# Two fused transformer blocks on one core: a weight split done by the load instead of by VectorE, and another order of work at the start of each feed-forward

## The reference, cut to what matters

```python
def swiglu(x, w_gate, w_up, w_down):
    return (jax.nn.silu(x @ w_gate) * (x @ w_up)) @ w_down

# first mixer: 8 heads, each with 64 columns without and 32 columns with rotation
q = (rms_norm(cq, q_norm_g) @ w_uq).reshape(B, S, MLA_HEADS, MLA_NOPE + MLA_ROPE)

# first block
f1 = swiglu(rms_norm(h, ffn1_pre_g[l]), ffn1_w_gate[l], ffn1_w_up[l], ffn1_w_down[l])
h = h + 0.5 * rms_norm(f1, ffn1_post_g[l])
...
f2 = swiglu(rms_norm(h, ffn2_pre_g[l]), ffn2_w_gate[l], ffn2_w_up[l], ffn2_w_down[l])
h = h + 0.5 * rms_norm(f2, ffn2_post_g[l])
```

## Time and profile before

| what | value |
|---|---|
| median of three runs | 1330.87 us |
| the profiled execution | 1330.87 us, its span 1329.2 us |
| TensorE (PE) busy | 1261.1 us, 95% |
| VectorE (DVE) busy | 789.1 us, 59% |
| ScalarE (ACT) busy | 593.7 us, 45% |
| GpSimd (POOL) busy | 453.0 us, 34% |
| mean granted TensorE clock | 0.970 of full |
| DMA | 206.98 MB, mean 156 GB/s |

### The profile page before, as it was taken

One profiled execution on the slowest core, in us unless ns is written; L12 is line 12 of the kernel. 1 busy time (PEld: TensorE's weight loads), 2 busy tenths in 40 slices (PEclk: granted clock), 3 DMA queues, 4 the chain that ended last, 5 costly groups with the idle time before them and its releaser, 6 DMA issues.

```text
span 1329.2 us, 23438 instructions
## 1 busy us (share of the span) xinstructions
PE 1261.1 (95%) x8728; PEld 1143.4 (86%) x8728; DVE 789.1 (59%) x1135; ACT 593.7 (45%) x976; POOL 453.0 (34%) x252
## 2 busy tenths in 40 slices
PE   6999999898999999999999999988999997999998
PEld 6999999866888999999998888866546797999998
DVE  6677764854974566666352944576324583755555
ACT  5444345525661454444435544343203533655553
POOL 0344334731460533333445642121000374122221
PEclk9999997998999999999969999999999999999999
DMA  8577753423334457777503323222212154455553
GB/s 331 206 267 260 263 197 106 143 95 111 101 107 126 160 182 246 273 280 258 184 17 127 127 94 113 86 89 80 79 63 95 65 176 141 143 180 184 185 178 110
DMA packets 58092, 206.98 MB, mean 156 GB/s; under 512 B 6576, under 2 KB 8240, under 8 KB 57776
## 3 DMA queue, kind: packets, MB, share of 16 engines
q1 hardware_dynamic: 49824, 177.23, 39.5%
q0 software_dynamic: 6912, 25.17, 5.4%
q10 hardware_dynamic: 1296, 3.74, 0.8%
HBM read 205.07 MB, written 1.05 MB: 155 GB/s over the span
## 4 chain that ended last, share of the span: by engine, by line
PE 78%; DVE 10%; DMA 4%; ACT 3%; issue 3%; POOL 1%; SPq 0%; ACTq 0%; DVEq 0%; POOLq 0%
PE psum L589 18%; PE psum L590 17%; PE psum L591 17%; PE psum L560 8%; DMA low<-stream 4%; PE psum L1190 2%; PE psum L915 2%; PE psum L719 2%; PE psum L610 1%; PE psum L1055 1%; ACT parts L1385 1%; POOL own_parts L2684 1%; DVE parts L1979 1%; DVE high L2158 1%; PE psum L1093 1%
## 5 line engine op out<-in xcount | busy, mean ns | idle before, releaser
L589 PE MATMUL psum<-parts 128*128 128x256 f32 x1584 | 452.9, 286 | 23.0 <-DVE parts L1985 11.2
L590 PE MATMUL psum<-parts 128*128 128x256 f32 x1584 | 450.7, 285 | 0.0
L591 PE MATMUL psum<-parts 128*128 128x256 f32 x1584 | 450.5, 284 | 0.0
L589 PEld LDWEIGHTS psum<-parts 128*128 128x128 f32 x1584 | 306.9, 194 | 25.8 <-issue 13.9
L590 PEld LDWEIGHTS psum<-parts 128*128 128x128 f32 x1584 | 306.8, 194 | 0.0
L591 PEld LDWEIGHTS psum<-parts 128*128 128x128 f32 x1584 | 306.6, 194 | 0.0
L1385 ACT ACTIVATE parts<-low 128x1024 fp32r<-128x1024 f32 x198 | 207.7, 1055 | 209.6 <-DMA low<-stream 202.2
L2692 POOL TENSOR_TENSOR parts<-low,parts 128x1024 fp32r<-128x1024 f32 x60 | 158.6, 2644 | 372.3 <-ACT parts L1385 372.3
L2684 POOL TENSOR_TENSOR own_parts<-low,parts 128x1024 fp32r<-128x1024 f32 x76 | 186.4, 2463 | 210.1 <-ACT parts L1457 205.9
L1979 DVE TENSOR_TENSOR parts<-low,parts 128x1024 fp32r<-128x1024 f32 x138 | 175.3, 1276 | 103.7 <-ACT parts L1385 103.4
L560 PE MATMUL psum<-low 128*128 128x256 f32 (+1 forms) x512 | 131.1, 410 | 1.2 <-ACT high L1470 1.2
(11 more groups left out here) (343 smaller groups left out, 1922.9 us busy)
## 6 DMA issues: line engine op xcount, KB each, us to landing
low<-stream SPq DMA_DIRECT2D x334, 512.0 KB, 3.5
high<-conditioning POOLq DMA_DIRECT2D x48, 512.0 KB, 5.8
high<-wuq ACTq DMA_DIRECT2D x1, 1152.0 KB, 11.0
low<-x SPq DMA_DIRECT2D x4, 256.0 KB, 5.6
high<-ctx ACTq DMA_DIRECT2D x1, 1024.0 KB, 6.2
out<-low SPq DMA_DIRECT2D x8, 128.0 KB, 1.8
low<-cst ACTq DMA_DIRECT2D x1, 850.5 KB, 4.7
low<-vec ACTq DMA_DIRECT2D x1, 157.5 KB, 5.9
```

The source lines that it names most:

```text
L589: pe.matmul(out, w_hi[:, cols_], x_hi, start=start, stop=False, **kw)
L590: pe.matmul(out, w_hi[:, cols_], x_lo, start=False, stop=False, **kw)
L591: return pe.matmul(out, w_lo[:, cols_], x_hi, start=False, stop=stop, **kw)
```

## The change

1. `w_nope` and `w_rope` become the two parts of the region of `wuq`, and two loads on ScalarE's queue write them, head by head, straight from memory. A row of `w_nope` is 24 runs of 256 bytes, a row of `w_rope` 24 runs of 128 bytes. VectorE's wait and its two copies go, and so does TensorE's wait for the last counts of `kv_scaled`; TensorE waits for three small loads (48) and not for two (32).
2. The four places of the state-space weights change (`WEIGHT_SUMS`).
3. At the start of each feed-forward, chunk 0: ScalarE's `upper` of tile 6 now stands ahead of `upper_hidden`, and VectorE's `lower` of tile 6 ahead of `lower_hidden`. Chunk 1 had that order already.
4. In feed-forward k = 1, `upper` of tiles 4 and 5 now stand between the root and the table load on ScalarE, and `lower` of tiles 4 and 5 before and after `invert` on VectorE. Before, tile 4 was done amid the first chunk's product, and tile 5 behind it.

```diff
+WEIGHT_SUMS = [ARENA_2["xdt"][0] + 2048, 0, ARENA_2["xdt"][0] + 3072, 0]
+for i in (1, 3):
+    WEIGHT_SUMS[i] = ARENA_2["mk"][0] + (WEIGHT_SUMS[i - 1] + 512 - ARENA_2["mk"][0]) % 1024 + 1024 * (i // 2)
...
-        w_nope = place(ARENA_1["p"][0], 3 * HEADS * NOPE).rearrange("p (k b) -> p k b", k=3)
-        w_rope = place(ARENA_1["va"][0], 3 * HEADS * ROPE_D).rearrange("p (k b) -> p k b", k=3)
+        w_flat, nopes = wuq.rearrange("p a b -> p (a b)"), 3 * HEADS * NOPE
+        w_nope, w_rope = (part.rearrange("p (k b) -> p k b", k=3) for part in (w_flat[:, 0:nopes], w_flat[:, nopes:]))
...
         both_ways = [place(at, 1024).rearrange("p (s t) -> p s t", s=4)
-                     for at in (ARENA_2["xdt"][0] + 2048, ARENA_2["xdt"][0] + 3072,
-                                ARENA_2["mk"][0], ARENA_2["mk"][0] + 1024)]
+                     for at in WEIGHT_SUMS]
...
-            pe.wait_ge(S("small_weights"), 32)
+            pe.wait_ge(S("small_weights"), 48)
...
-            pe.wait_ge(S("kv_scaled"), 4)
...
                     gate(par, par, k > 0, 0)
-                    if par == 0:
-                        upper_hidden(par, FC * k + par)
-                        if k == 1:
-                            upper(1, 5)
                     upper(k, 6 + 3 * par)
-                    if par == 1:
-                        upper_hidden(par, FC * k + par)
+                    upper_hidden(par, FC * k + par)
...
-            act.dma_start(wuq, dram["wuq"]).then_inc(S("small_weights"), 16)
+            w_heads = dram["wuq"].rearrange("p k (h c) -> p (k h) c", h=HEADS)
+            for part, own in ((w_nope, slice(0, NOPE)), (w_rope, slice(NOPE, NOPE + ROPE_D))):
+                act.dma_start(part.rearrange("p k (h c) -> p (k h) c", h=HEADS),
+                              w_heads[:, :, own]).then_inc(S("small_weights"), 16)
...
             take_root("ffn2_pre", D)
+            uppers(1, 4, RING)
             act.preload_act_table(ACT.Silu)
             copy_inverse("ffn2_pre", inv)
-            upper(1, 4)
...
                     product(par, par, 0)
-                    if par == 0:
-                        lower_hidden(par, FC * k + par)
-                        if k == 1:
-                            lower(1, 5)
                     lower(k, 6 + 3 * par)
-                    if par == 1:
-                        lower_hidden(par, FC * k + par)
+                    lower_hidden(par, FC * k + par)
...
-                    if k == 1 and isinstance(f, int) and f == 0:
-                        lower(1, 4)
...
-            dve.wait_ge(S("small_weights"), 32)
-            w_heads = wuq.rearrange("p k (h c) -> p (k h) c", h=HEADS)
-            for part, own in ((w_nope, slice(0, NOPE)), (w_rope, slice(NOPE, NOPE + ROPE_D))):
-                dve.tensor_copy(part.rearrange("p k (h c) -> p (k h) c", h=HEADS), w_heads[:, :, own])\
-                   .then_inc(S("kv_scaled"), 1)
...
             input_sums("ffn2_pre", sq)
+            lower(1, 4)
             invert("ffn2_pre")
+            lower(1, 5)
```

More of the change, by code:

```diff
@@ L200 @@
     ("t0", 512), ("tc", 1024), ("rowm", 512), ("rowl", 256)], END_COMMON)
+WEIGHT_SUMS = [ARENA_2["xdt"][0] + 2048, 0, ARENA_2["xdt"][0] + 3072, 0]
+for i in (1, 3):
+    WEIGHT_SUMS[i] = ARENA_2["mk"][0] + (WEIGHT_SUMS[i - 1] + 512 - ARENA_2["mk"][0]) % 1024 + 1024 * (i // 2)
+assert WEIGHT_SUMS[3] + 1024 <= ARENA_2["mo"][0]
 ATT, _ = regions([("aq", 1024), ("ak", 2048), ("av", 2048), ("after_av", 16), ("mo", 1024), ("ya", 1024)],
@@ L213 @@
 assert END_1 + DC * T <= END_2
-assert 3 * HEADS * NOPE <= 2048 and 3 * HEADS * ROPE_D <= 1024
 HEADS_M = END_2
```

## The result

| | median of the runs | ratio to before, 95% interval |
|---|---|---|
| before, in this comparison | 1332.62 us (1328.63 to 1335.74, 4 runs) | |
| changed | 1346.73 us (1343.40 to 1351.78, 4 runs) | 1.0103 [1.0060, 1.0146] |
| changed, measured again with 9 runs | 1342.48 us, beside 1331.54 for before | 1.0089 [1.0059, 1.0119] |
| forecast | 1335.5 us, range 1329.0 to 1343.0 | 1.0035 |

The change makes the kernel slower by about 1%. The first median lies above the range; that of the 9 runs lies just inside it, at its upper end, and both are two to three times the forecast's +4.6 us away from before. The profiled execution of the changed kernel took 1338.22 us (span 1336.6), less than any of its four timed runs.

The account below looks back on a forecast made before the run. TensorE was taken as the bound, 78% of the chain of work. 1330.87 + 1.8 (loads) + 0 + 2.3 (k = 1) + 0.5 (k = 2) = 1335.5 us, +0.35%, range 1329.0 to 1343.0.

Parts of the forecast that it names:

- The two loads, +1.8 us: Before 36.3 us: new loads delay stream tiles 8 and 9, lengthening TensorE's wait; +1.8 us, bounds -2.2 and +3.4.
- the third rival: ScalarE stands at issuing `w_rope` or `wkr`, ahead of the first feed-forward's root; 6 to 8 us, total 1341; chance 0.12.
- The stream stands still behind the new loads: After 17 us: stream tiles queue behind the new loads' descriptors, SyncE's queue empty for several us, tile 9 late.
- The size of short runs: New loads' 6144 runs at 18 ns each, an estimated 14 for the shorter half; engines held 6.1 us, 3.4 more.
- The rival of dear short runs: Short runs of the new loads cost far more than their bytes, holding engines 11 us; total 1342; chance 0.06.
- The copies, 0: At 270.22 us: VectorE's two copies, 1.42 us, lie wholly in cover of TensorE's product; removing them gains 0.
- k = 0, 0: First feed-forward: `lower_hidden` some 1.2 us later, but TensorE's 2.2 us wait further on takes the delay whole; 0 more.
- k = 1, +2.3 us: Second feed-forward: early tiles and tile 6 delay `lower_hidden` to 483.9 and TensorE's unbroken stretch to 484.0; +2.3 us.
- k = 2, +0.5 us: Last feed-forward: `lower_hidden` 1.2 us later, TensorE has about 0.8 us to spare; 0.5 us lost.
- The places, 0: State-space products: both column halves already run side by side, so new addresses give 0, with 0.3 us either way.
- The clock: Rival: longer idle before 36.3 us and idle stretches in k = 1 lower the clock; 1337.1 or 1338.7 us; chance 0.20.
- theory D: From the experiments: excess comes from loads' traffic meeting the new order; table-change hold plus new order would cost +5 to +6 us.

Follow-up runs that it names:

- e1_loads: Kernel before with only the two head-by-head loads in place of one load and VectorE's copies; 1339.11 us, ratio 1.0032.
- e4_late_rope: Kernel before with the two head-by-head loads and no copies, `wkr` issued first and `w_rope` only after the first feed-forward; 1334.39 us, ratio 0.9996.
- e13_held: Kernel before plus eight changes of ScalarE's table between its loads and the first feed-forward's root, no more bytes moved; 1335.72 us, ratio 1.0035.
- e11_loads_again: Repeat of the kernel before with only the two head-by-head loads in place of one load and the copies; 1339.02 us, ratio 1.0049.
- e5_laid_out: Kernel before without the copies and their wait, query weights laid out head by head in DRAM for one load; 1333.33 us, ratio 1.0009.
- e9_after_again: The whole changed kernel, measured again against the kernel before with 9 runs; 1342.48 us, ratio 1.0089.
- e3: Kernel before with only the new places of the state-space weights; 1333.05 us, ratio 0.9985.
- e14: Kernel before with VectorE's conditioning products in the first two feed-forwards cut to 64 of 1024 columns; 1332.43 us.
- e2_order: Kernel before with only the new order of tiles 4, 5 and 6 at the feed-forwards' starts; 1336.51 us, ratio 1.0008.
- e17_light_order: Kernel before with the new tile order and conditioning products cut to 64 of 1024 columns; 1333.97 us, +1.5 us against e14.
- light kernels: Kernel before, changed, loads alone and order alone, conditioning products cut to 64 of 1024 columns; 1332.43, 1340.42, 1337.37 and 1333.97 us.

## Why the prediction was wrong, by its steps

- **The two loads, +1.8 us: this step failed.** It let ScalarE issue both loads freely and put their whole cost on the stream. The runs showed ScalarE held for 9.36 us at the second issue and 2.52 at the next (7.9 and 4.2 in `e1_loads`), TensorE idle for 9.9 us, and 4 to 7 us of that kept (+4.0, +5.1 and +4.9 us timed, 5.8 to 7.1 by the matmuls done at 45 us). It is the third rival, given 0.12: its mechanism, its place and its sign ("one of these issues takes over 1.6 us") came true. That its price of 6 to 8 us came near is in part luck: it had the root at 24.5 to 27 and not at 29.29, and the delay kept whole, where 3.6 us of waits took up a part. It was weighed down by a row that did not bear on it: with three loads unfinished, the issues of the earlier trace rows were short, but those loads had few runs, where `w_nope` has 3072. The count that decided it, 24 times as many descriptors in front, stood in the working, and was used for the stream alone.
- **The stream stands still behind the new loads: not seen.** The DMA queues of the changed kernel from 17.2 to 20.9 us, and then from 24 to 27 us:

```profile
q10 hardware_dynamic: 221, 0.83, 81.2%
q1 hardware_dynamic: 19, 0.08, 6.5%
```
```profile
q10 hardware_dynamic: 1401, 0.36, 54.1%
q1 hardware_dynamic: 142, 0.50, 46.5%
```

  In the first stretch the stream all but stands, as it did before, beside packets of 3.8 KB on average. While the short runs pass, both queues move at once, and with TensorE late no tile was late for it. In `e4_late_rope`, with `w_nope` in the queue and no hold, waits of 1.9 us up to 45 us stand for the 3.6 of before. So the delay of tiles 8 and 9 took the standstill beside large packets for something that short ones would bring about too.
- **The size of short runs: right.** 0.541 x 16 x 3 / 1401 = 18.5 ns for a run of 257 bytes on average, as in the earlier trace rows; forecast 18. The rival of dear short runs is out with it, and with the time of `e4_late_rope`. `e13_held` beside `e11_loads_again` (1.0035 and 1.0049, intervals that overlap) could hide a few us of traffic. The Trainium skill ("DMA: Bandwidth & Descriptors", Specifications) has runs under 512 B read, modified and written, and below line rate. The second agrees: 257 bytes in 18.5 ns is 13.9 bytes a ns, and 9216 bytes in 335 ns is 27.5, twice that. How a short run is written, no trace shows.
- **The copies, 0: right.** The earlier trace rows had the cover, VectorE waits for it longer now, and `e5_laid_out` gives 1.0009.
- **k = 0, 0: no cost seen, but the cover that was named is gone.** The wait of 2.2 us ahead of tile 9 is no longer there. At 45 us `e11_loads_again` (part 1) and `e9_after_again` (the whole) both have 140 matmuls done. Without a hold the traces can't tell 1.2 us, 10 matmuls: with the old order and the early loads they have 180 to 199 done (before, e3, e5, e14), with the new one 178 (`e2_order`) and 196 (`e17_light_order`).
- **k = 1, +2.3 us: 1.9 measured,** in the changed kernel and in `e2_order`, by the steps described: uppers behind the root, the first `lower` ahead of the reciprocal, the copy at 482.29. The spread waited 1.2 us, not 1.5.
- **k = 2, +0.5 us: right.** `lower_hidden` is 1.2 us later, and TensorE waits 0.4 us for it where it had no wait; that is one trace, too small for the runs to confirm.
- **The places, 0: right.** 1.95 us a group in both, and 0.9985 [0.9960, 1.0010] for `e3_places`.
- **The clock: its own rival did not come true.** No new low stretch in k = 1. The one at 36 us moved to 22.4 us and covers TensorE's restart up to 36.05; what it costs more, 1.1 us, is part of the 7.1 us.
- **What was missing altogether** is how much the runs of one kernel differ: lone traces cannot tell 3 us here, since the turns in which GpSimd lies over VectorE's product come and go.

With +1.8 replaced by the 6.5 us of the light kernels, and 1.9 and 0.5 for the rest, the sum is +8.9 us, 1339.8. That is the light kernels' difference, and it lies inside the intervals of the whole (1.0059 and 1.0060 are +7.9 and +8.0 us), but at their lower end: what separates it from the +11 to +14 us of the medians is not settled. The turns with the longer product can make 6.7 us between one execution of the changed kernel and another, but counted over 14 kernels they are no more frequent with a late start than without, so they explain the scatter and not the gap; and theory D, the loads' traffic meeting the new order, is not excluded: the light kernels leave 1.6 us for it by the medians, give or take 3.

## What to carry to other kernels

Count the descriptors (the separate runs of bytes) that stand ahead of an issue in its own queue, not only the bytes: here a load of 3072 short runs was issued in 0.6 to 0.8 us, and the next issue of that queue paid, with every computation behind it on that engine. The kernel before had more bytes ahead of `wkr`, 1152 KB in 128 runs, and issued it in 0.45 us. How many runs it takes between 128 and 3072 was not measured. Put such a load last on its queue, ahead of nothing that the bound engine waits for, or issue it in a stage where its engine is idle. And before a copy is bought off with a load, look whether it costs anything: here 1.42 us in full cover were traded for a hold of 12 us.

## What the runs showed of the hardware

- **An issue that blocks.** In seven traces the issue behind a load of 3072 runs takes 7.0 to 9.4 us, and the one behind both 2.5 to 4.6, where `w_rope` takes 0.57 with nothing ahead and `wkr` 0.45 to 1.33 with few runs ahead. The blocked one, 9.36 us long, began 0.7 us after the one ahead, and ScalarE came free within 0.2 us of that one's landing, 12.1 to 13.2 us after its issue. The Trainium skill ("DMA: Bandwidth & Descriptors", Issuing engines are not separate DMA queues) calls the sequencer's time for an issue "usually small relative to the DMA itself"; here it was 9.36 us, beside the 13.7 us to the landing of the same load.
- **A hold of 9.9 us costs 4 to 7.** TensorE made up its waits of 3.6 us, and 7.5 of the 13.65 us of low clock fell into idle time.
- **VectorE beside GpSimd.** A group of products on 128 x 1024 grows by 2.2 us when a GpSimd subtraction of 2.7 us lies over it. Between 1 and 14 of 16 groups were long, from one profiled execution to the next, with no relation to the late start to be seen.
